# Splitting GEMM weights into high and low part two blocks at a time

## The reference

```python
h = jnp.matmul(_rmsnorm(x, norm_g), w_in)      # layer 1 and 2, 2048 x 8192: ab_in, c_in
return x + jnp.matmul(y, w_out)                # layer 1 and 2, 2048 x 2048: ab_out, c_out
pk = hc @ w_in[l][:, OFF_K:]                   # layer 3, context rows: ctx
pl = hl @ w_in[l]                              # layer 3: lat
x_lat = x_lat + m_lat[2] * (y_l @ w_out[l])    # mix_out
q = ht @ wq                                    # expert query: wq
m = jax.nn.silu(cond) @ w + b                  # the modulation: 2048 x 12288, two condition vectors
```

## Time and profile before

| what | us |
|---|---|
| median of 3 runs | 3710.57 (3707.09 to 3721.67) |
| span of the profiled execution | 3716.1 |
| PE busy | 3182.8 |
| DVE busy | 2600.6 |
| ACT busy | 1438.5 |
| eight GEMM stages together, some | 1400 |

### The profile page before, as it was taken

How to read it: one execution, slowest core, us unless ns; L and a number is a source line. 1 busy time by engine, 2 the same in 40 slices (tenths; PEclk the granted TensorE clock), 3 DMA queues, 4 the chain that set the end, 5 groups by cost and what they waited for, 6 DMA issues and landing times. The chain is left out here.

```text
span 3716.1 us, 48967 instructions
## 1 busy us (share of the span) xinstructions
PE 3182.8 (86%) x12442; PEld 2221.2 (60%) x12442; DVE 2600.6 (70%) x4845; ACT 1438.5 (39%) x2767; POOL 374.4 (10%) x484
## 2 busy tenths in 40 slices
PE   5999749899968695996875907999999999999997
PEld 4888737788836584885664802222222278888885
DVE  6888468776737746554465498999999955555555
ACT  4555224555524435554244501111111145555553
POOL 0000110000030000000000002333333300000000
PEclk9999769999968896997787955555555599999998
DMA  5888209688706551663033407999999955555553
GB/s 205 290 289 290 72 23 333 224 291 288 277 12 233 188 158 33 194 192 102 6 120 115 142 0 299 379 380 371 379 379 370 368 204 191 192 192 192 192 191 126
DMA packets 213914, 787.68 MB, mean 212 GB/s; under 512 B 18514, under 2 KB 19666, under 8 KB 151250
## 3 DMA queue, kind: packets, MB, share of 16 engines
q1 hardware_dynamic: 159904, 407.33, 32.5%
q0 software_dynamic: 50688, 369.12, 26.5%
q10 hardware_dynamic: 3250, 10.41, 0.8%
HBM read 781.55 MB, written 5.24 MB: 212 GB/s over the span
## 5 line engine op out<-in xcount | busy, mean ns | idle before, releaser
L384 DVE TENSOR_TENSOR w_lo<-raw,w_hi 128x512 fp32r<-128x512 f32 x1008 | 671.4, 689 | 387.0 <-ACT w_hi L356 386.7
L356 ACT ACTIVATE w_hi<-raw 128x512 fp32r<-128x512 f32 x1008 | 632.8, 632 | 726.5 <-PE bank L375 664.5
L373 PE MATMUL bank<-w_hi,xt_hi 128*128 128x512 f32 x2016 | 795.4, 395 | 61.6 <-DVE w_lo L384 61.6
L374 PE MATMUL bank<-w_lo,xt_hi 128*128 128x512 f32 x2016 | 792.1, 393 | 0.0
L375 PE MATMUL bank<-w_hi,xt_lo 128*128 128x512 f32 x2016 | 791.4, 393 | 0.0
L1398 DVE CUSTOM_DVE_ANT_0 u_ring<-u_ring,bank 128x1024 f32<-128x1024 f32 x512 | 600.7, 1206 | 12.4 <-DMA u_ring<-in_peer_u,idx 10.0
L1470 DVE TENSOR_TENSOR w_lo<-v_raw,w_hi 128x512 fp32r<-128x512 f32 x512 | 354.4, 693 | 299.2 <-ACT w_hi L1454 299.2
L1342 PE MATMUL bank<-row_ring,three 3*128 3x512 bf16 x1024 | 527.0, 616 | 33.7 <-DVE act_in L1398 9.5
L373 PEld LDWEIGHTS bank<-w_hi,xt_hi 128*128 128x128 f32 x2016 | 383.0, 190 | 148.5 <-DVE w_lo L384 68.6
L1454 ACT ACTIVATE w_hi<-v_raw 128x512 fp32r<-128x512 f32 x512 | 323.3, 632 | 332.3 <-PE bank L1492 328.1
L375 PEld LDWEIGHTS bank<-w_hi,xt_lo 128*128 128x128 f32 x2016 | 382.9, 190 | 80.2
(11 more groups left out here) (300 smaller groups left out, 2551.8 us busy)
## 6 DMA issues: line engine op xcount, KB each, us to landing
v_raw<-in_peer_v SPq DMA_DIRECT2D x128, 1024.0 KB, 4.7
ada_ring<-in_ada_w POOLq DMA_DIRECT2D x96, 1024.0 KB, 5.3
raw<-in_w_in_ab SPq DMA_DIRECT2D x128, 512.0 KB, 5.0
raw<-in_w_in_c SPq DMA_DIRECT2D x128, 512.0 KB, 4.5
raw<-in_w_in SPq DMA_DIRECT2D x120, 512.0 KB, 3.7
raw<-in_w_out_ab SPq DMA_DIRECT2D x32, 512.0 KB, 7.7
raw<-in_w_out_c SPq DMA_DIRECT2D x32, 512.0 KB, 7.7
raw<-in_w_out SPq DMA_DIRECT2D x32, 512.0 KB, 4.5
```

The costliest lines, as they stand in the source:

```text
L356: act.activation(w_hi[:, kk % WS, :], raw[:, q % RAW, kk % KC, :], ACT.Copy).then_inc(hi_ready, 1)
L373: pe.matmul(o, a_hi, b_hi, start=kk == 0, stop=False)
L374: pe.matmul(o, a_hi, b_lo, start=False, stop=False)
L384: dve.tensor_tensor(w_lo[:, kk % WS, :], raw[:, kk // KC % RAW, kk % KC, :], w_hi[:, kk % WS, :].bitcast(F32), ALU.subtract).then_inc(raw_ ...
```

## The change

ACT and DVE handle two chunks (one `raw` slot) by one instruction of 1024 columns instead of two of 512. The ring keeps its four chunks. ACT now waits, ahead of chunks kk and kk + 1, until PE has finished chunk kk - 3, where it waited for kk - 4 ahead of chunk kk. The semaphores count by two. PE and SP are as before.

```diff
                     if before and kk == WS:
                         take_h(act, g, n - 1, 1 - s)
-                    q = kk // KC
                     if kk % KC == 0:
+                        q = kk // KC
                         act.wait_ge(w_landed[q % RAW], 16 * (g["c0"] // RAW + Q // RAW * n + q // RAW + 1))
-                    act.wait_ge(chunk_multiplied, PRE + g["c0"] * KC + K * n + kk - WS + 1)
-                    act.activation(w_hi[:, kk % WS, :], raw[:, q % RAW, kk % KC, :], ACT.Copy).then_inc(hi_ready, 1)
+                        act.wait_ge(chunk_multiplied, PRE + g["c0"] * KC + K * n + kk - WS + KC)
+                        act.activation(w_hi[:, kk % WS:kk % WS + KC, :], raw[:, q % RAW, :, :], ACT.Copy).then_inc(hi_ready, KC)
...
             def low(n, kk):
-                dve.wait_ge(hi_ready, PRE + g["c0"] * KC + K * n + kk + 1)
-                dve.tensor_tensor(w_lo[:, kk % WS, :], raw[:, kk // KC % RAW, kk % KC, :],
-                                  w_hi[:, kk % WS, :].bitcast(F32), ALU.subtract).then_inc(raw_used, 1)
+                dve.wait_ge(hi_ready, PRE + g["c0"] * KC + K * n + kk + KC)
+                dve.tensor_tensor(w_lo[:, kk % WS:kk % WS + KC, :], raw[:, kk // KC % RAW, :, :],
+                                  w_hi[:, kk % WS:kk % WS + KC, :].bitcast(F32), ALU.subtract).then_inc(raw_used, KC)
...
                 for kk in range(K):
-                    low(n, kk)
+                    if kk % KC == 0:
+                        low(n, kk)
                     if kk == WS - 1 and before and take:
                         evacuate(n - 1, 1 - s)
                     if kk % 4 == 3 and ada:
```

## The result

The changed kernel takes 3816.5 us (median of 4 runs) against 3708.8 us (median of 4 of the kernel before, taken with it): a ratio of 1.0289, 95% interval 1.0262 to 1.0317. Forecast was 3805 us with a range of 3770 to 3845. The profiled spans are 3813.6 and 3716.1 us, 97.5 us apart.

What follows compares the result with a forecast made beforehand. PE was taken to bound the GEMM stages, with ACT and DVE having time to spare. Terms 28 + 28 + 24 + 4.5 + 7 + 2 = 94 us on the median of 3710.6 gave 3805 us, range 3770 to 3845.

Steps and rivals of the forecast that it cites:

- The second rival: In the GEMM stages, the DVE time saved by wide subtractions reaches the end: 77 us less, 3634 us; chance 1%.
- The first rival: The wide subtraction on DVE takes about 0.7 us, so only take-outs stall: some 3725 us; chance 4%.
- Modulation in c_in: DVE's multiply-add between subtractions stalls PE each time, 0.83 us or 1.01 in a tile's first quarter: 28 us.
- The new chain, without other work: From PE's start on a pair, ACT and DVE have the next ready at 2.68 us, under the 2.72 covered.
- Modulation in ab_in: Modulations two pairs apart: the first stall of 0.83 us pays for both, so every second of 64 costs: 28 us.
- Lat, ctx and wq: Stages without modulation: next to nothing lost, 2 us in all, for pairs that wake late.
- rival 3: Chain longer than cover, at 2.83 us; some 350 of 504 pairs lose 0.11 us each: 40 us, 3845 us; chance 12%.
- ab_out and c_out: Stalls after take-outs and modulations, 9.4 us per stage, plus 3 for late DMAs: 12 us each, 24 in all.
- Fills: Start of each of eight stages: chain longer by 0.43 us on ACT and 0.54 on DVE, 7 us in all.
- rival 4: PE's gaps let its clock fall to 1.2 GHz in parts of c_in or ab_in: 70 us more, 3875 us; chance 3%.
- Rival 5: Stalls exist, but DMAs set the end of ab_out and c_out, so nothing is added there: 3781 us; chance 8%.
- The sign posts: PE's idle time at L373 for DVE's `w_lo` rises from 61.6 us to some 150, in more than 60 pieces.

Runs made afterwards that it cites:

- the last kernel: The kernel before, narrow instructions, with each multiply-add of the modulation done twice, one after the other: 3938.6 us, ratio 1.0625.

## Why the prediction was right, point by point

- **PE bounds the stages, the saved time on ACT and DVE is worth nothing**: right. DVE's L384 and ACT's L356 are busy 56 and 99 us less, and nothing came of it. The longer idle times of both are in the profile after. The second rival, that the saving reaches the end, has nothing for it. The errata section of the Trainium skill's page "VectorE: DVE Perf Modes" is right on the duration (1223 ns against twice 689), and here does not carry to the time of the kernel, as DVE waits for others.
- **Durations of 1.06 and 1.226 us**: 1060 and 1223 ns. The first rival, a fast subtraction, is out.
- **Modulation in c_in, 28 us**: 31 gaps with most at 0.8 and 1.0 us. With the small gaps removed the stage is 29 us longer than before. In the changed kernel it was 34. The other 5 are the small gaps, and here the step that failed is "The new chain, without other work": it had the starts of before, 0.20 and 0.03 us, where 0.26 and 0.10 were measured, so that the chain is 2.81 us and not 2.68, over the cover instead of under it.
- **Modulation in ab_in, one of two stalls pays for both**: the sum is right (some 31 us of gaps with the small ones, as in c_in with half the modulations), its form is not. There are 62 gaps of 0.1 to 1.0 us rather than 31 whole ones: the stall is shared between two neighbours.
- **Lat, ctx and wq, 2 us in all**: measured 8.7. A mis-sized term, from the same chain: 0.06 us per pair in lat. It is what rival 3 had described, and its chain of 2.83 us was nearly right, though it had other terms in mind. Its price was not: it charged the whole excess to every pair, where the ring of two pairs makes it half.
- **ab_out and c_out, 12 us each**: 7.3 and 7.4. The gaps are there: 0.8 us after a modulation alone, 1.6 to 1.9 after the take-outs in ab_out and 1.2 to 1.7 in c_out. But some 3 us of gaps by late DMAs that PE had suffered before went away rather than grew. ACT waited 22.1 us for weights in c_out before and 4.9 now. The stage is slower, which gives the DMAs time, but that is not the whole of it: the wait is down to 7.1 us already in the kernel with the coarse wait alone, whose c_out took 94.0. Taking the 3 with the other sign would have been right.
- **mix_out, 4.5 us**: three gaps of 1.4 to 1.5 us, as said; the stage is 6.7 us longer, with the small gaps.
- **Fills, 7 us**: right as far as it shows. The fill is 0.99 us longer in each of the four late stages, where 0.97 was said, but none of it is in the 97 us of the stages.
- **The sum, 94 us**: 97.5 us between the spans, 107.7 between the medians, which differ from the spans' difference by the scatter of single runs. The measured stages are 34 + 33 + 7 + 7 + 7 + 9 = 97, and with the fills 104. That the sum came so close is in part luck: 9 us too much in ab_out and c_out made up for nearly half of the 20 us that the terms of the other stages were short of.
- **The clock** (rival 4): 0.98 to 0.99 in all stages. With gaps of up to 1 us in every 11, no fall was seen.
- **Rival 5**, nothing added in ab_out and c_out: out, with 7.3 and 7.4 us there.
- **The sign posts**: idle time of PE at L373 of "some 150 in more than 60 pieces" came out as 118.1 in 97, since a short gap is partly hidden in that row. Reading the starts of successive matmuls is the surer way.

## What to carry to other kernels

In a ring between three engines, first write down the cover (what the consumer still has when the producer is released) and the chain (wake, work, wake, work, wake), and only then the widths: a wider instruction cuts the cover and lengthens the chain at once, and saves only on engines that may not be waited for. Then look for the longest thing that ever stands in the middle engine's queue; it is that one, not the average load, that must fit between chain and cover. If it doesn't, deepen the ring or cut the long instruction, unless the cut asks for a DMA's data earlier in a stage that its DMAs bound.

## What the runs showed of the hardware

- An instruction that adds two to its semaphore starts later after the wait in front of it: 0.10 us instead of 0.03 on DVE, 0.26 instead of 0.20 on ACT (means over lat, on ACT from PE's release). It was tried both ways on both engines. The trace shows a separate wait of 17 or 21 ns ahead of each such instruction, and 45 ns from its end to the instruction's start.
- Where the chain of the producers is longer than the cover of a ring of two pairs, each pair loses about half of the excess: 0.04 us of gap for 0.09.
- The 1024-column conversion takes 1060 ns against 632 for 512 columns, and the subtraction 1223 against 689.
- PE's granted clock stayed at 0.99 in a stage with 62 gaps of up to 1 us, and at 0.99 in c_in of the last kernel, with 31 gaps of 1.8 to 2.0 us.
